# Gate logits by eight stacked matmuls, and the stores of the transposed tiles issued by SyncE, in the first stage of a two-layer hybrid decoder

## The reference

```python
h = jnp.concatenate([meta, x], axis=1)                       # 16 + 2048 tokens of 1024
xn = rmsnorm(h, norm_g)
proj = xn @ w_in
b_logit = proj[..., GDN_QKV_W + GDN_VAL_W:GDN_QKV_W + GDN_VAL_W + GDN_HEADS]
a_logit = proj[..., GDN_QKV_W + GDN_VAL_W + GDN_HEADS:]
beta = jax.nn.sigmoid(b_logit)
g = -jnp.exp(a_log) * jax.nn.softplus(a_logit + dt_bias)
```

## Time and profile before

| what | value |
|---|---|
| median of 3 runs | 2793.78 us (2791.85 to 2794.45) |
| the profiled execution | 2792.86 us, its span 2790.9 us |
| PE busy over the span | 2501.1 us (90%) |
| DVE, ACT, POOL busy | 1675.1 us (60%), 1137.0 us (41%), 456.7 us (16%) |
| first stage, to the first DMA of the second | 119.36 us |
| DMA in the whole span | 392.79 MB, mean 141 GB/s |
| PE's granted clock, mean over the span | 0.957 of full speed |

### The profile page before, as it was taken

How to read it: one execution, slowest core, us unless ns; L and a number is a source line. 1 busy time by engine, 2 the same in 40 slices (tenths; PEclk the granted TensorE clock), 3 DMA queues, 4 the chain that set the end, 5 groups by cost and what they waited for, 6 DMA issues and landing times. The chain is left out here.

```text
span 2790.9 us, 50427 instructions
## 1 busy us (share of the span) xinstructions
PE 2501.1 (90%) x17193; PEld 2195.6 (79%) x17193; DVE 1675.1 (60%) x3904; ACT 1137.0 (41%) x3326; POOL 456.7 (16%) x345
## 2 busy tenths in 40 slices
PE   5568888899999999999999689999997999999997
PEld 4467777789998999999999568878885777777775
DVE  4367676677777777777777333333332667666664
ACT  4244454544444444444444244433332233333332
POOL 0133343210000000000000012100001333323331
PEclk8689999999999999999999689999997999999998
DMA  6664354544445444444353067643455222222221
GB/s 190 204 246 143 138 170 148 176 133 132 141 139 186 140 146 124 133 151 136 120 171 97 22 205 254 243 157 140 180 199 232 68 69 85 85 69 75 68 69 48
DMA packets 273814, 392.79 MB, mean 141 GB/s; under 512 B 79282, under 2 KB 187906, under 8 KB 273442
## 3 DMA queue, kind: packets, MB, share of 16 engines
q1 hardware_dynamic: 240066, 370.05, 39.9%
q10 hardware_dynamic: 33632, 21.26, 2.6%
HBM read 267.92 MB, written 123.31 MB: 140 GB/s over the span
## 5 line engine op out<-in xcount | busy, mean ns | idle before, releaser
L1229 PE MATMUL p_psp<-xg,p_whi 128*128 128x264 f32 x4096 | 846.0, 296 | 26.2 <-POOL p_wlo L1178 17.2
L1229 PEld LDWEIGHTS p_psp<-xg,p_whi 128*128 128x128 f32 x4096 | 658.2, 192 | 30.8 <-issue 21.5
L1229 PE MATMUL p_psp<-xg,p_wlo 128*128 128x264 f32 x2048 | 608.2, 297 | 0.0
L1229 PEld LDWEIGHTS p_psp<-xg,p_wlo 128*128 128x128 f32 x2048 | 392.9, 192 | 0.0
L981 DVE SCALAR_TENSOR_TENSOR p_acc<-p_proj,p_taps,p_acc 128x528 f32<-128x528 f32 x288 | 250.8, 871 | 4.6
L1824 PE MATMUL first_q<-first_w,p_o 128*128 128x512 f32 (+1 forms) x864 | 206.5, 398 | 16.3 <-DVE first_w L1788 16.3
L2366 PE MATMUL first_q<-first_w,p_hT 128*128 128x512 f32 x720 | 196.8, 413 | 13.9 <-DVE p_q L2252 13.5
L1824 PEld LDWEIGHTS first_q<-first_w,p_o 128*128 128x128 f32 (+1 forms) x864 | 156.8, 184 | 59.2 <-issue 14.2
L2366 PE MATMUL p_pso<-p_wo,p_oT 128*128 128x512 f32 x768 | 194.4, 404 | 7.9 <-DVE p_oT L2278 4.2
L862 ACT ACTIVATE p_sig<-p_sig 128x528 f32<-128x528 f32 x128 | 82.7, 646 | 291.5 <-DVE p_sig L983 291.4
L2366 PEld LDWEIGHTS p_pso<-p_wo,p_oT 128*128 128x128 f32 x768 | 143.7, 192 | 48.7 <-issue 16.1
(11 more groups left out here) (263 smaller groups left out, 4655.9 us busy)
## 6 DMA issues: line engine op xcount, KB each, us to landing
p_whi<-w_dram SPq DMA_DIRECT2D x92, 512.0 KB, 4.1
p_wlo<-w_dram SPq DMA_DIRECT2D x92, 512.0 KB, 4.8
raw<-w_a_in SPq DMA_DIRECT2D x36, 512.0 KB, 6.3
w_dram<-p_whi SPq DMA_DIRECT2D x34, 512.0 KB, 4.1
w_dram<-p_wlo SPq DMA_DIRECT2D x34, 512.0 KB, 5.2
p_o<-hT_dram SPq DMA_DIRECT2D x34, 512.0 KB, 4.9
hT_dram<-p_hT SPq DMA_DIRECT2D x32, 512.0 KB, 3.4
p_hT<-hT_dram SPq DMA_DIRECT2D x30, 512.0 KB, 4.1
```

The source lines that it names most:

```text
L1229: ins = nc.tensor.matmul(ps_p[half_][:, 0:HALF], (w_hi, w_lo)[i][:, f, kc * P:(kc + 1) * P], xg[:, g % 2, j, kc, half_ * HALF:(half_ + 1) ...
```

## The change

Three things are edited, all in the first stage.

The high and low parts of a tile lie side by side in one tensor, and so do those of the gate weights (32 stationary columns: 16 high, 16 low). One matmul for each slice of features takes 32 columns of weights and 256 moving columns (128 tokens of the high part, 128 of the low part). PSUM then holds four blocks: rows 0 to 15 high weights, rows 16 to 31 low weights, the left half by the high part of the tokens, the right half by the low part. `keep_logits` copies the left half and adds the right half to it, with a wait between the two. The 17 transposes at the end become 17 float32 matmuls with two stacked 16x16 identities as moving operand, which turn and add the two row blocks at once. (The product low by low, which was left out before, is now in the sum.) Two more small DMAs fetch the stacked identities ahead of the first loads of tokens.

The two stores of tiles 5 to 16 are issued by SP and no longer by ACT. SP issues them for tile T-4 behind the load of tile T; the last four tiles follow after the last load.

```diff
-        x_hi = sb("p1_hi", [P, 2, KC, P], f32r)
-        x_lo = sb("p1_lo", [P, 2, KC, P], f32r)
+        x_s = sb("p1_xs", [P, 2, 2, KC, P], f32r)
+        part_sum = sb("p1_part_sum", [4 * H, 2 * H])
-        wba_s = [sb(f"p1_wba{n}", [P, KC * 2 * H], f32r) for n in range(2)]
+        wba_s = sb("p1_wbas", [P, KC, 2, 2 * H], f32r)
-        logitsT = sb("p1_logitsT", [2 * H, NTT, P])
+        logitsT = sb("p1_logitsT", [4 * H, NTT, P])
-        N_CONST = 8
+        N_CONST = 10
...
+        def both_of(T, slot, rows, kc):
+            if in_place(T):
+                first = 0 if T == 0 else META + (T - 1) * P
+                return xg[:, 0, :, kc, first:first + rows]
+            return x_s[:, slot, :, kc, 0:rows]
...
-                             (dt_row[:], dt_bias.partition_broadcast(P))):
+                             (dt_row[:], dt_bias.partition_broadcast(P)),
+                             (part_sum[0:2 * H, :], consts["ident"][0:2 * H, 0:2 * H]),
+                             (part_sum[2 * H:4 * H, :], consts["ident"][0:2 * H, 0:2 * H])):
...
+            def store(T, slot):
+
+                tok = bass.ds((T - 1) * P + META, P)
+                sp.wait_ge(hi_ready, 2 * (T + 1))
+                sp.dma_start(xT_d[0][:, :, tok], x_s[:, slot, 0].bitcast(f32)).then_inc(stored[slot], 16)
+                sp.wait_ge(lo_ready, 2 * (T + 1))
+                sp.dma_start(xT_d[1][:, :, tok], x_s[:, slot, 1].bitcast(f32)).then_inc(stored[slot], 16)
+
             load_group(0)
-            with sp.Fori(1, NG) as g:
-                load_group(g)
+            load_group(1)
+            with sp.Fori(2, NG) as g:
+                for c in range(TPG):
+                    slot = (c + 1) % 2
+                    sp.wait_ge(xn_ready, TPG * g + c)
+                    sp.dma_start(x_sb[:, slot, :], x[bass.ds((TPG * g + c) * P, P), :]).then_inc(x_in[slot], 16)
+                    store(TPG * g + (c - 3), slot)
+            for T in range(NT - TPG + 1, NT + 1):
+                store(T, T % 2)
...
-                if in_place(T):
-                    return
-                tok = bass.ds((T - 1) * P + META, P)
-                act.wait_ge(hi_ready, 2 * (T + 1))
-                act.dma_start(xT_d[0][:, :, tok], x_hi[:, slot].bitcast(f32)).then_inc(stored[slot], 16)
-                act.wait_ge(lo_ready, 2 * (T + 1))
-                act.dma_start(xT_d[1][:, :, tok], x_lo[:, slot].bitcast(f32)).then_inc(stored[slot], 16)
...
             def keep_logits(T, slot, rows):
+
                 dve.wait_ge(lg_ps, T + 1)
-                dst = logitsT[:, T, 0:rows] if isinstance(T, int) else \
-                    logitsT[:].rearrange("p t k -> p (t k)")[:, bass.ds(T * P, P)]
-                nc.vector.tensor_copy(dst, ps_l[slot][0:2 * H, 0:rows]).then_inc(lg_read, 1)
+                flat = logitsT[:].rearrange("p t k -> p (t k)")
+                dst = logitsT[:, T, 0:rows] if isinstance(T, int) else flat[:, bass.ds(T * P, P)]
+                both = ps_l[slot][0:4 * H, 0:2 * rows].rearrange("p (n k) -> p n k", n=2)
+                nc.vector.tensor_copy(dst, both[:, 0, :]).then_inc(lg_kept, 1)
+                dve.wait_ge(lg_kept, T + 1)
+                nc.vector.tensor_tensor(dst, both[:, 1, :], dst, ALU.add).then_inc(lg_read, 1)
...
-                parts = [p for kc in range(KC) for p in split_parts(kc)]
-                for n, (i, j, kc) in enumerate(parts):
-                    last = nc.tensor.matmul(ps_l[slot][0:2 * H, 0:rows], wba_s[i][:, kc * 2 * H:(kc + 1) * 2 * H],
-                                            split_of(T, slot, rows, j)[:, kc],
-                                            start=n == 0, stop=n == len(parts) - 1)
+                for kc in range(KC):
+                    last = nc.tensor.matmul(ps_l[slot][0:4 * H, 0:2 * rows].rearrange("p (n k) -> p n k", n=2),
+                                            wba_s[:, kc].rearrange("p n m -> p (n m)"), both_of(T, slot, rows, kc),
+                                            start=kc == 0, stop=kc == KC - 1)
...
             for T in range(NTT):
-                last = nc.tensor.transpose(ps_l[0][:, T * 2 * H:(T + 1) * 2 * H], logitsT[:, T, :],
-                                           ident[0:2 * H, 0:2 * H])
+                last = nc.tensor.matmul(ps_l[0][:, T * 2 * H:(T + 1) * 2 * H], logitsT[:, T, :], part_sum[:],
+                                        start=True, stop=True)
```

More of the change, by code:

```diff
@@ L89, in normalise_and_transpose @@
         lg_read = sem("p1_lg_read")
+        lg_kept = sem("p1_lg_kept")
         lgT_ps = sem("p1_lgT_ps")
@@ L118, in split_of @@
                 return xg[:, 0, part, :, first:first + rows]
-            return (x_hi, x_lo)[part][:, slot, :, 0:rows]
+            return x_s[:, slot, part, :, 0:rows]
+        def both_of(T, slot, rows, kc):
[3 more added lines that the diff above has]
+            return x_s[:, slot, :, kc, 0:rows]
         @block.sync
@@ L198, in _ @@
             nc.scalar.activation(a_neg[:], a_neg[:], ACT.Exp).then_inc(a_exp, 1)
-            nc.scalar.activation(wba_s[0][:], wba[:], ACT.Copy).then_inc(wba_hi, 1)
+            nc.scalar.activation(wba_s[:, :, 0], wba[:].rearrange("p (c m) -> p c m", c=KC), ACT.Copy).then_inc(wba_hi, 1)
             stats(1, 1, 0, P)
@@ L265, in _ @@
             dve.wait_ge(wba_hi, 1)
-            nc.vector.tensor_tensor(wba_s[1][:], wba[:], wba_s[0][:].bitcast(f32), ALU.subtract).then_inc(wba_lo, 1)
+            nc.vector.tensor_tensor(wba_s[:, :, 1], wba[:].rearrange("p (c m) -> p c m", c=KC),
+                                    wba_s[:, :, 0].bitcast(f32), ALU.subtract).then_inc(wba_lo, 1)
             norm(1, 1, P, True)
```

## The result

The changed kernel takes 2802.21 us (median of 9 runs, 2797.63 to 2808.37) beside 2794.89 us for the kernel before (9 runs); the ratio of the runs compared is 1.0025, 95% interval 1.0016 to 1.0033. That is inside the predicted range of 2790.0 to 2803.0 and on the side predicted, 7 us slower where 3 were forecast. But the sum does not add up as it was put: in the two profiles the first stage became 14.9 us longer, not 2.9, and 6.8 us of that were given back in the second stage, where nothing was edited.

What follows compares the result with a forecast made beforehand. It took a chain of engines to bound the early tiles and, from tile 5, the same chain beside nearly full DMA engines. -0.7 + 5.5 - 3.7 + 0.3 + 1.5 = +2.9 us on 2793.78 gave 2796.7 us, range 2790.0 to 2803.0.

Steps and rivals of the forecast that it cites:

- Up to norm(7): Early tiles, until tile 7's normalising: cheaper logits matmuls less the add and new constants, -0.7 us, bounds -1.8 and +0.7.
- The moved stores: Normalising of tile 7 to tile 15: high parts wait for later-issued stores to land, +5.5 us, bounds +1.9 and +9.9.
- rival of the longer landing: Tiles 7 to 14 and 16: stores land 8.5 us after norm(t), not 7.0; +10.4 us, 2804; chance 2 in 10.
- that of the low clock: Logits matmuls: PE stays at the lower clock, logits take 2.0 us; +6.4 us, 2800.2; chance 1 in 10.
- The end: Normalising of tile 15 to the copy of tile 16's logits: -3.7 us, bounds -4.7 and -2.0.
- The turns: First stage's end: float32 matmuls in place of 17 transposes, 17 more instructions; +1.5 us, bounds +0.5 and +2.4.
- The sum of the first stage: All first-stage terms together: the second stage's first DMA shifts by +2.9 us, with L720 near 122.
- The prediction's last sentence: Behind the first stage: if L720 shifts otherwise than the total time, something there moved.
- The full queue (faster): Tile loop: each tile costs only its bytes, 4.9 us; -4.7 us in all, 2789.1; chance 2 in 10.
- The rule that was weighed: Moved stores: DMAs from different engines share the same 16 DMA engines, so the issuing engine saves only issue time.
- the estimate of 5.6 us: Load and two stores of a tile, by about 2.0 us and bytes over 436 GB/s; 5.6 us instead of 6.9.

Runs made afterwards that it cites:

- one_more_dve: The kernel before with one more DVE instruction per tile in `keep_logits` (a maximum that changes no values), PE and stores as before; 2794.3 us, ratio 1.0005.
- gates_only: Against the changed kernel, the stores are back on ACT; the stacked matmuls, the add and the float32 turns stay; 2791.5 us, ratio 0.9992 to the kernel before.
- early_store: The changed kernel, but SP issues the stores of tile T-3 behind the load of tile T, one tile earlier; 2787.5 us, ratio 0.9981 to the kernel before.
- four_slots: The changed kernel with four slots in place of two for the parts of tiles 5 to 16, tile loops written out; 2786.3 us, ratio 0.9976 to before.
- moved_code: The kernel before with 13 tiny unused DVE memsets in the first microseconds, shifting DVE's later code; 2785.4 us, ratio 0.9968.
- best: four_old_gates with 20 tiny DVE memsets at the start, which shift DVE's later code; 2780.9 us, ratio 0.9953 to the kernel before.
- four_old_gates: Against four_slots: the 24 matmuls, no add and transposes as in the kernel before; four slots and stores from SP stay; 2790.2 us, ratio 0.9987 to before.

## Why the prediction was right or wrong

**Up to norm(7): right in size.** -0.2 us for -0.7 predicted. The eight matmuls take 1.1 us at the higher clock and 2.06 at the lower, as worked out from the 264-column rows. The new constants cost 0.25 us of delay to norm(0) (9.44 beside 9.19), not 0.9. But the add seems to cost more than the 0.33 us a tile that was taken (one_more_dve: 48.6 us for eight tiles beside 43.5 to 46.0 in kernels with the same matmuls, so 0.3 to 0.6), and it ate the gain of the matmuls (gates_only: 43.4 beside 43.5).

**The moved stores: mechanism right, two sizes low.** (95.98 - 42.53) - (86.27 - 42.73) = +9.9 us for +5.5, at the end of the bounds given. From norm(t)'s end to high_part(t) it is 7.3 to 7.5 us for odd tiles and 7.6 to 8.3 for even ones, where 7.0 was taken. From there to norm(t+2)'s end it is 5.8 to 5.9 us for 5.25 in six of eight tiles, 6.2 and 6.6 in the others: the logits take 1.92 us since PE stays at its lower level, which the forecast had split evenly. So the rival of the longer landing and that of the low clock were both partly there. early_store and four_slots show the wait for the slot to be the cause.

**The end: -1.4 us for -3.7.** From norm(15)'s start to the copy of tile 16's logits, 14.7 us where it was 16.1. norm(16) ended 6.5 us after norm(15), not 5.0, again the low clock and the landing.

**The turns: mis-sized, +6.2 us for +1.5.** The step that failed says "17 more of at least 0.07". The price of a transpose was carried over to a float32 matmul, though the earlier trace rows have two float32 instructions in 0.82 us, and the upper bound of +2.4 was made from them by taking off a price of their columns that no row gives. (17 times 0.07 is 1.2, too; the rest of the +1.5 has no source.) Measured: 0.22 us for each of 34, in four kernels alike (7.43 us), where a transpose of the same rows takes 0.12 at the same lower clock. The 0.07 was also read at the higher clock, and the turns of the changed kernel ran at the lower one.

**The sum of the first stage: wrong.** -0.2 + 9.9 - 1.4 + 0.3 + 6.2 = +14.8 us for +2.9. L720 was to be issued near 122 us and its line was at 134.2; the copy of tile 16's logits was to start near 104 and started at 110.7. The prediction's last sentence asked for a look behind the stage if the first DMA and the total moved apart, and that is what happened.

**What was not in the prediction: DVE's code.** The adds put 13 instructions more into DVE's program. That alone is worth about 9 us of the kernel before (moved_code), and in the two profiles 6.8 us came back. The time fell inside the range because this gain hid about half of a loss five times the forecast: 2794.9 + 14.8 would be 2809.7 us, outside it. That the number came out right was luck. Beside moved_code, with its code at the same place, the change costs 1.0025 / 0.9968 = 1.0057, 16 us (give or take 4, an estimate from the two intervals), and their first stages differ by 134.2 - 117.4 = 16.8 us.

**The rivals.** The full queue (faster) did not come about in the change, since a store can't leave before norm(t), as argued; it did in four_slots, at 5.1 us a tile where it named 4.9. The longer landing was to decide from 7.7 us on; by its own prices (4.0 us in the tiles and 1.0 at the end for each us) that should read 7.5, which odd tiles nearly reached and even ones passed. The rule that was weighed (the Trainium skill, DMA: Bandwidth & Descriptors, "Issuing engines are not separate DMA queues") is borne out as to the transfers, since one queue carried what two did; it says nothing on who waits for them, and the place in SP's order cost 10 us. The Trainium skill's figure for one DMA (DMA: Bandwidth & Descriptors, "Anatomy of one DMA") is stated for DMAs that GpSimd issues, while SP issued these; the estimate of 5.6 us from it was low, 7.3 to 8.3 was measured.

## What to carry to other kernels

A store that frees a buffer has a place in an order, and moving it to another engine moves that place: count from when it is issued to when its slot is wanted, and issue it a tile earlier or give it more slots. Price a float32 matmul from rows of float32 matmuls at the same clock, not from transposes. And when an edit changes how many instructions an engine's program has, compare the stages that were not edited: a few idle instructions in a place where the engine waits anyway tell a gain or loss of code position from one of the edit.

## What the runs showed that was not expected

- The position of DVE's code in front of the second stage's loop is worth 0.3% of this kernel: by the count of the expectation of best, 121 instructions ahead of it (before) or 114 (four_old_gates) give 14 to 16 packets of q14 in 320 us and two waits of 3.3 to 3.5 us at the state update; 131 to 138 give 5 or 6 and no such wait. (The traces give two fewer for every kernel, with the loop counted once and semaphore waits left out.)
- One such wait is followed by a stretch of lower clock on PE: after the 4.8 us stand near 437 us the lag of the changed kernel's DVE instructions behind the same ones of before shrank from 14.6 to 9.8 us by 446. A shorter stand is followed by one in one place and not in another: moved_code has a clock of 0.66 from 430 to 435 us behind a stand of PE of 2.4 us that ends at 429.3, the changed kernel has 1.00 behind one of 2.4 us that ends at 450.1.
- With loads and stores on one queue the first stage moves 305 to 319 GB/s from 60 to 80 us (four_slots, four_old_gates), no less than on two (294 and 312 in the kernel before).
- A second DVE instruction of 128 columns, 0.33 us behind its copy, made eight tiles 2.6 to 5.1 us longer (one_more_dve beside moved_code and before), 0.3 to 0.6 us a tile; where what goes beyond the 0.33 us comes from stayed open.
- The stacked matmuls go with a lower granted clock of PE at the turns: 0.50 in all seven kernels that have them, 1.00 in all seven with the 24 matmuls.
